# Conditioning rows spread by TensorE, spectra products 1024 wide, first units of up in another order

## The reference

```python
mod_x = silu(c) @ w_mod + b_mod          # and mod_c = silu(c_ctx) @ w_mod + b_mod
h = modulate(rms_norm(x, g_pre_mix), sh_m, sc_m)
x = x + gt_m * rms_norm(merge_heads(attention, retention, gate) @ w_out, g_post_mix)
x = x + gt_f * rms_norm((silu(a) * b) @ w_ffn_out, g_post_ffn)
# second block
x0, x1, v = split(short_conv(h @ w_in + b_in, sc_w, sc_b))
y = irfft(rfft(x1 * v) * rfft(kern)) + x1 * v * bias
x = x + g1 * ((x0 * y) @ w_out + b_out)
x = x + g2 * (silu(dwconv3x3(g)) * a) @ w_down      # a, g = split(modulate(rmsnorm(x)) @ w_up)
out = rmsnorm(x, final_g)
```

## Time and profile before

| | |
|---|---|
| median of three runs | 1423.12 us |
| profiled execution | 1426.7 us |
| its span, first to last instruction | 1424.9 us |
| TensorE busy | 1377.7 us, 97% |
| VectorE busy | 931.9 us, 65% |
| ScalarE busy | 540.2 us, 38% |
| GpSimd busy | 97.4 us, 7% |
| mean granted TensorE clock | 0.993 |

### The profile page before, as it was taken

How to read it: one execution, slowest core, us unless ns; L and a number is a source line. 1 busy time by engine, 2 the same in 40 slices (tenths; PEclk the granted TensorE clock), 3 DMA queues, 4 the chain that set the end, 5 groups by cost and what they waited for, 6 DMA issues and landing times.

```text
span 1424.9 us, 17227 instructions
## 1 busy us (share of the span) xinstructions
PE 1377.7 (97%) x6376; PEld 1102.7 (77%) x6376; DVE 931.9 (65%) x1277; ACT 540.2 (38%) x792; POOL 97.4 (7%) x119
## 2 busy tenths in 40 slices
PE   7899999999999999999999999999999999999996
PEld 5688887666888888888886577778887888888885
DVE  6756587786386666664134896999478888885222
ACT  3523253555462232323222654333453333333221
POOL 0002631000210000000110000000200000000010
PEclk9899999999999999999999999999999999999999
DMA  9434431032307565564521022220222322233311
GB/s 377 150 105 137 137 92 43 15 118 82 125 17 277 211 218 214 214 247 180 161 90 48 30 92 72 75 103 30 91 73 89 103 88 92 100 120 102 102 61 59
DMA packets 44803, 168.83 MB, mean 118 GB/s; under 512 B 5547, under 2 KB 6123, under 8 KB 43852
## 3 DMA queue, kind: packets, MB, share of 16 engines
q1 hardware_dynamic: 43340, 165.21, 33.2%
q0 software_dynamic: 1408, 2.89, 0.7%
HBM read 163.09 MB, written 2.10 MB: 116 GB/s over the span
## 4 chain that ended last, share of the span: by engine, by line
PE 81%; DVE 12%; ACT 2%; DMA 2%; issue 2%; SPq 0%; POOL 0%; DVEq 0%; ACTq 0%; POOLq 0%
PE PS L649 64%; PE PS L942 2%; PE PS L1009 2%; DVE tb L2060 2%; DVE wsp L639 1%; DVE sink L2116 1%; DVE H L2060 1%; PE PS L1204 1%; DMA mfirst<-mod_x 1%; PE PS L1301 1%; PE PS L1272 1%; DMA mring<-mod_c 1%; PE PS L1000 1%; PE PS L907 1%; DVE ca L2060 1%
## 5 line engine op out<-in xcount | busy, mean ns | idle before, releaser
L649 PE MATMUL PS<-H,wsp 128*128 128x512 f32 x3216 | 744.5, 392 | 12.1 <-DVE wsp L639 8.2
L649 PEld LDWEIGHTS PS<-H,wsp 128*128 128x128 f32 x3216 | 601.3, 188 | 148.8 <-DVE wsp L639 10.6
L639 DVE TENSOR_TENSOR wsp<-wraw,wsp 128x1024 fp32r<-128x1024 f32 (+1 forms) x172 | 223.1, 1299 | 335.0 <-ACT wsp L632 334.3
L632 ACT ACTIVATE wsp<-wraw 128x1024 fp32r<-128x1024 f32 (+1 forms) x172 | 191.8, 1118 | 468.8 <-PE PS L649 460.5
L649 PE MATMUL PS<-hid,wsp 128*128 128x512 f32 x1056 | 240.0, 389 | 0.0
L649 PEld LDWEIGHTS PS<-hid,wsp 128*128 128x128 f32 x1056 | 198.2, 188 | 41.7 <-issue 0.6
L2060 DVE SCALAR_TENSOR_TENSOR cva<-PS,dert,cva 128x441 f32<-128x441 f32 (+2 forms) x176 | 122.2, 694 | 5.5
L2262 DVE CUSTOM_DVE_ANT_0 sink<-mring,crow_t,colt 128x1024 bf16<-128x1024 f32 x56 | 71.8, 1281 | 11.4 <-DMA mring<-mod_c 10.8
L1969 POOL COPY acc<-sqb 128x512 f32<-128x512 f32 x4 | 3.9, 972 | 850.0 <-ACT sqb L1345 305.9
L1972 POOL TENSOR_TENSOR acc<-acc,sqb 128x512 f32<-128x512 f32 x20 | 34.1, 1707 | 184.3 <-ACT sqb L1947 82.6
L1690 ACT ACTIVATE hid<-hv 128x512 f32 (+1 forms) x22 | 13.9, 632 | 81.2 <-DVE hv L2535 81.2
(11 more groups left out here) (333 smaller groups left out, 1490.8 us busy)
## 6 DMA issues: line engine op xcount, KB each, us to landing
mring<-mod_c SPq DMA_DIRECT2D x56, 512.0 KB, 4.7
wraw<-w_ffn_in SPq DMA_DIRECT2D x44, 512.0 KB, 3.7
wraw<-w_up SPq DMA_DIRECT2D x44, 512.0 KB, 3.5
wraw<-w_hy_in SPq DMA_DIRECT2D x24, 512.0 KB, 3.5
wraw<-w_w_in SPq DMA_DIRECT2D x22, 512.0 KB, 3.5
wraw<-w_ffn_out SPq DMA_DIRECT2D x16, 704.0 KB, 4.0
wraw<-w_down SPq DMA_DIRECT2D x16, 704.0 KB, 4.0
mfirst<-mod_x SPq DMA_DIRECT2D x12, 512.0 KB, 16.6
```

What stands on the lines that cost most here:

```text
L632: nc.scalar.activation(split_parts(name, i, r)[0], wraw[:, g % RAW, 0:n], ACT.Copy).then_inc(w_hi, 1)
L639: nc.vector.tensor_tensor(part_lo, wraw[:, g % RAW, 0:n], part_hi.bitcast(F32), ALU.subtract).then_inc(w_lo, 1)
L649: mm = nc.tensor.matmul(psum, wsp[:, o % 2, a, wk * P:(wk + 1) * P], h[:, b, kt, :], start=first and kt == kts[0] and (a, b) == (0, 0), st ...
```

## The change

Three edits that don't touch each other.

At the start SP issues one row of each of the two conditioning rows to a single partition (`crow_r`, 8 KB), then `ones`, then `colt`. TensorE multiplies the first row of `ones` (a column of 1/1024 for each partition) by that row, four matmuls of 512 columns, which puts the rows divided by 1024 on all partitions in four PSUM banks; ScalarE's silu reads them with a scale of 1024. VectorE's work is the same.

In the spectra the product is made as four operations, two of 1024 columns, in which the filter's real or imaginary part is read twice by a stride of zero, and two of 512. The final sums are two of 1024 columns.

In the first units of up the sum over the second half's squares is split: tile 6's stands after two channel tiles, tile 7's after three, where both stood after five. ScalarE takes the root of the second half after all eight high parts of the first, spreads the splits of units 2 and 3 among the high parts of the second half, and loads the table of silu at the end. VectorE adds the residual of tile 7 one step earlier.

```diff
+        crow_r = sb("crow_r", o_r + 66 * K, [1, 2, D])
...
-        zp = [zA[:, 0, :], zA[:, 1, :], sb("zp2", o_t + 11 * K, [P, 512]), sb("zp3", o_t + 13 * K, [P, 512])]
+        zB = sb("zB", o_t + 11 * K, [P, 2, 512])
...
+        def spectra(c, f, pair):
+
+            return KS[:, c, (1, 0, 2, 3)[2 * f + pair], :, :]
...
+            sp.dma_start(crow_r[:, :, :], crow[0:1, 0:3:2]).then_inc(s_crow, 16)
+            sp.dma_start(ones[:, :], mats[0]).then_inc(s_crow, 16)
             sp.dma_start(colt[:, :], cols).then_inc(s_cols, 16)
-            for v in range(2):
-                sp.dma_start(crow_t[:, v, :], crow[:, 2 * v]).then_inc(s_crow, 16)
...
-            sp.dma_start(ones[:, :], mats[0]).then_inc(s_small, 16)
...
+            pe.wait_ge(s_crow, 32)
+            for b in range(4):
+                nc.tensor.matmul(PS[:, b, :], ones[0:1, :], crow_r[0:1, b // 2, b % 2 * 512:b % 2 * 512 + 512],
+                                 start=True, stop=True).then_inc(c_row, 1)
             pe.wait_ge(silu_c, 1)
             for m in range(3):
                 modulation(m)
-            pe.wait_ge(s_small, 16)
             squares_total(0)
...
-            def half_total(half):
+            def half_total(half, tiles=(6, 7)):
 
                 cs, bank = half_of(half * KT), 6 - half
-                pe.wait_ge(n_acc, acc_base(6) + 6)
-                nc.tensor.matmul(PS[:, bank, 0:HL], ones[:, :], acc[:, cs], start=True, stop=False)
-                for n in (6, 7):
+                if tiles[0] == 6:
+                    pe.wait_ge(n_acc, acc_base(6) + 6)
+                    nc.tensor.matmul(PS[:, bank, 0:HL], ones[:, :], acc[:, cs], start=True, stop=False)
+                for n in tiles:
...
                 pe.wait_ge(o_ev, 8)
-                tiles(range(0, 5), 0)
-                half_total(1)
-                tiles(range(5, KT), 0)
+                tiles(range(0, 2), 0)
+                half_total(1, (6,))
+                tiles(range(2, 3), 0)
+                half_total(1, (7,))
+                tiles(range(3, KT), 0)
                 tiles(range(KT), 1)
...
-            act.wait_ge(s_crow, 32)
             for v in range(2):
-                SC.activation(crow_t[:, v, :], crow_t[:, v, :], ACT.Silu).then_inc(crow_on, 1)
+                act.wait_ge(c_row, 2 * v + 2)
+                SC.activation(crow_t[:, v, :], PS[:, 2 * v:2 * v + 2, :].rearrange("p a b -> p (a b)"),
+                              ACT.Silu, scale=float(D)).then_inc(crow_on, 1)
...
             half_root(0)
-            half_highs(0, 3)
+            half_highs(0, 2)
             half_out(7, 1)
-            half_highs(3, 4)
+            half_highs(2, 4)
             half_square(7, 1)
-            half_highs(4, 6)
+            half_highs(4, KT)
             half_root(1)
-            half_highs(6, KT)
+            half_highs(KT, KT + 4)
             split_hi(act, "up", 2, after=ORD["hy_out"] + 7)
+            half_highs(KT + 4, 2 * KT)
             split_hi(act, "up", 3, after=ORD["hy_out"] + 8)
-            half_highs(KT, 2 * KT)
+            SC.preload_act_table(ACT.Silu)
...
-                z_re, z_im = zs[:, 2 * d, :], zs[:, 2 * d + 1, :]
-                k_re, k_im = spectrum(k // 2, f, 2 * d), spectrum(k // 2, f, 2 * d + 1)
-                re, im = zp[2 * d][:, :], zp[2 * d + 1][:, :]
-                VE.tensor_tensor(re, z_re, k_re, ALU.mult)
-                own(VE.tensor_tensor(im, z_im, k_im, ALU.mult))
-                VE.tensor_tensor(re, re, im, ALU.subtract)
-                VE.tensor_tensor(z_re, z_re, k_im, ALU.mult)
-                own(VE.tensor_tensor(z_im, z_im, k_re, ALU.mult))
-                own(VE.tensor_tensor(z_re, z_re, z_im, ALU.add))
+                z, y = zs[:, 2 * d:2 * d + 2, :], (zA, zB)[d]
+                k_re, k_im = [spectrum(k // 2, f, 2 * d + part).unsqueeze(1).to_broadcast([P, 2, 512])
+                              for part in range(2)]
+                VE.tensor_tensor(y[:, :, :], z, k_re, ALU.mult)
+                own(VE.tensor_tensor(z, z, k_im, ALU.mult))
+                VE.tensor_tensor(y[:, 0, :], y[:, 0, :], z[:, 1, :], ALU.subtract)
+                own(VE.tensor_tensor(y[:, 1, :], y[:, 1, :], z[:, 0, :], ALU.add))
...
-                VE.tensor_tensor(to[0], zp[0][:, :], zp[2][:, :], ALU.add)
-                VE.tensor_tensor(to[2], zp[0][:, :], zp[2][:, :], ALU.subtract)
-                VE.tensor_tensor(to[1], zs[:, 0, :], zs[:, 2, :], ALU.add)
-                VE.tensor_tensor(to[3], zs[:, 0, :], zs[:, 2, :], ALU.subtract).then_inc(z_y, 1)
+                VE.tensor_tensor(to[0], zA[:, :, :], zB[:, :, :], ALU.add)
+                VE.tensor_tensor(to[1], zA[:, :, :], zB[:, :, :], ALU.subtract).then_inc(z_y, 1)
...
                 half_low(i0 + 1)
+                if i0 == 0:
+                    half_residual(7, 1)
                 for i in range(i0 + 2, i0 + KT):
                     if i + 2 < i0 + KT:
                         half_scaled(i + 2)
                     half_low(i)
-                    if i == 2:
-                        half_residual(7, 1)
```

More of the change, by code:

```diff
@@ L267, in build @@
         s_crow = sem("s_crow")
+        c_row = sem("c_row")
         s_hyc = sem("s_hyc")
@@ L2177, in _ @@
             scaled(1, Xc, "a_ctx", (0, 1, 2, 3), LC)
-            dve.wait_ge(s_small, 64)
+            dve.wait_ge(s_small, 48)
             own(VE.tensor_tensor(centre[:, :], ident[:, :], bones[:, :], ALU.subtract))
@@ L2693, in z_products @@
                 f = k % 2
-                z_re, z_im = zs[:, 2 * d, :], zs[:, 2 * d + 1, :]
-                k_re, k_im = spectrum(k // 2, f, 2 * d), spectrum(k // 2, f, 2 * d + 1)
-                re, im = zp[2 * d][:, :], zp[2 * d + 1][:, :]
-                VE.tensor_tensor(re, z_re, k_re, ALU.mult)
-                own(VE.tensor_tensor(im, z_im, k_im, ALU.mult))
-                VE.tensor_tensor(re, re, im, ALU.subtract)
-                VE.tensor_tensor(z_re, z_re, k_im, ALU.mult)
-                own(VE.tensor_tensor(z_im, z_im, k_re, ALU.mult))
-                own(VE.tensor_tensor(z_re, z_re, z_im, ALU.add))
-            def z_final(k):
-                to = [spectrum(k // 2, k % 2, part) for part in range(4)]
-                VE.tensor_tensor(to[0], zp[0][:, :], zp[2][:, :], ALU.add)
-                VE.tensor_tensor(to[2], zp[0][:, :], zp[2][:, :], ALU.subtract)
-                VE.tensor_tensor(to[1], zs[:, 0, :], zs[:, 2, :], ALU.add)
-                VE.tensor_tensor(to[3], zs[:, 0, :], zs[:, 2, :], ALU.subtract).then_inc(z_y, 1)
+                z, y = zs[:, 2 * d:2 * d + 2, :], (zA, zB)[d]
[5 more added lines that the diff above has]
+                own(VE.tensor_tensor(y[:, 1, :], y[:, 1, :], z[:, 0, :], ALU.add))
+            def z_final(k):
+                to = [spectra(k // 2, k % 2, pair) for pair in range(2)]
+                VE.tensor_tensor(to[0], zA[:, :, :], zB[:, :, :], ALU.add)
+                VE.tensor_tensor(to[1], zA[:, :, :], zB[:, :, :], ALU.subtract).then_inc(z_y, 1)
                 dve.wait_ge(z_y, k + 1)
```

## The result

The changed kernel took 1417.94 us (median of seven runs, 1415.8 to 1420.34), the kernel before 1424.73 in the same comparison (seven runs, 1422.78 to 1427.13). The medians differ by 6.8 us. The ratio is 0.995, with a 95% interval of 0.9941 to 0.9959, which is 7.1 us, 5.8 to 8.4. The forecast was 1416.9.

The account below looks back on a forecast made before the run. TensorE was taken to bound the kernel with 81% of the chain of waits, VectorE 12%. Start 1.5, spectra 1.7 and up 3.0 sum to 6.2 us, from the median of 1423.12 to 1416.9; range 1413.9 to 1420.4.

Parts of the forecast that it names:

- the 1074.5: Up's end: TensorE's long last piece, at 1078.18 before, starting later than this would show the forecast wrong.
- the start: Program start: VectorE reaches the unit it waited for at 20.07 instead of 21.55; gain 1.5 us.
- up: First units of up: shorter `tiles`, hidden table load, VectorE setting the wait for unit 5; gain 3.0 us, bounds 1.8 and 4.3.
- the price of the four products: Start: TensorE's four new float32 products, priced by the first four sums over squares, take 5.8 us.
- The first rival: Start: TensorE's rate stays at 1.71 us for all four products, the start gives nothing, 1418.4 us; chance 0.17.
- The landing's term: Start: the matrix's next unit lands 2.0 to 2.9 us earlier, taken as 2.2, so at 19.35.
- The transfer term: Start: the small transfer `ones`, issued at 1.21, lands at 3.9, at most about 4.1.
- The spectra: Between 884 and 982 us: each product takes VectorE 0.25 less, final sums 0.12 less; gain 1.7 us.
- The term of `tiles`: First units of up: first `tiles` matmul to the next full unit takes 15.5 us instead of 17.3; 1.8 gained.
- The bound of 4.3: First units of up: the upper bound of the gain, with TensorE ready for unit 5 at 1073.9.
- The operand that is read slowly: Spectra rival: a stride of zero halves VectorE's rate, 12.8 us more, 1429.7 us; chance 0.04.
- The clock's fall: Rival: TensorE's lower clock moves onto the chain or lasts longer, costing 3.4 us, 1420.3 us; chance 0.08.

Follow-up runs that it names:

- rows_12: Changed kernel with eight more one-row products behind the four at the start, into free banks; 1428.06 us in one run, the kernel before 1427.32 beside it.
- rows_full: Changed kernel with the four start products over all 128 rows, 127 of them zero; 1420.81 us in one run, the kernel before 1427.32 beside it.
- rows_apart: Changed kernel with VectorE taking the first row's sums of its first three units before the second row's; 1418.53 us (0.9946), again 1419.45 (0.9954).

## Why the prediction was right, and where it was off

The time came out 1.0 us above the forecast and in its range, and the sign and the places were right. As a gain it was 6.8 us by the medians for 6.2, since the kernel before took 1.6 us more in this comparison than the median from which the forecast started. The three places in the trace give 7.07. TensorE's long last piece starts at 1069.31, well before the 1074.5 that would have shown the forecast wrong, but 1.8 of that is the part that no edit gave. Two terms had the wrong size, in opposite directions: the start gave 0.9 less than forecast and up 1.6 more. That the sum came so close is in part luck.

**The start (forecast 1.5, traced 0.63, timed nothing).** The step that failed is the price of the four products, 1.71 + 1.71 + 1.49 + 0.86. It was taken from sums over 128 rows, in which TensorE's rate rose; in products with one active row it didn't (`rows_12`, `rows_full`), and four took 7.2. That VectorE and not the landing then decides, and that some 9.32 us lie between its start and the unit that it had waited for, held: 20.93 less 11.71 is 9.22. The first rival had the mechanism: rate unchanged through all four and hardly anything gained. Its sign, a start of VectorE's after 12, did not show, because `ones` came early and made up for part of it. The landing's term was somewhat too large: in the three profiles in which it can be seen the landing came 1.96, 1.63 and 1.41 earlier than in the kernel before, for 2.2 with a lower bound of 2.0. The transfer term erred to the other side: `ones` came 1.86 after its issue, not 2.7. The Trainium skill, DMA: Bandwidth & Descriptors, under "Anatomy of one DMA", has a fixed cost of about 2.0 us. The trace about agrees, with 1.86.

**The spectra (1.7, traced 1.88).** Right in each step: 3.72 a product, 1.22 for an operation with the spread operand, no surcharge, and the 0.68 in front of the inverse transform just fitted. Its second half was forecast for 979.1. Its start can't be seen in a row of 128 matmuls, but the unit behind it starts 4.34 earlier than before (991.74 for 996.08), which puts it at 978.01. Of the 4.34, 0.63 come from the start, 1.83 from the stretch without edits and 1.88 from the spectra.

**Up (3.0, traced 4.56).** The term of `tiles` was mis-sized, 15.5 where 13.74 was measured. I priced a matmul by a piece of the chain, 1.77 us for 12, 0.1475 each; the 78 in one run take 10.17, 0.130 each. 96 at 0.130 and three sums are 13.8. So in the kernel before some 3.6 us of the 17.31 went to waits and to what each break adds to the matmuls around it, not 1.8, and all of that went. Its timeline shows four waits there, of which the prediction read one, the 1.22 of the earlier trace rows. The others are

```profile
1044.79 1.77 PE L1009 MATMUL PS<-H,upw 128*128 128x256 f32 x12 [0.15 <-DVE H L2060]
...
1052.48 0.98 PE L1009 MATMUL PS<-H,upw 128*128 128x256 f32 x6 [1.01 <-DVE H L2060]
...
1053.67 5.58 PE L1009 MATMUL PS<-H,upw 128*128 128x256 f32 x42 [0.21 <-DVE H L2060]
```

and the last row, 42 in 5.58 or 0.133 each, would have given the right price. The order of waits held: silu at once, VectorE in front of unit 5, a wait of 1.58 for 1.3. With 3.57 for `tiles` instead of 1.8, the same steps give 3.57 + 1.28 = 4.85, less the 0.25 by which the load is not hidden: 4.6, and 4.56 came through. The bound of 4.3 fell with it, since it too was counted from 1.8. VectorE sets it, but 1.6 us earlier than forecast.

**The other rivals.** The operand that is read slowly is out (1.22). The clock's fall did move between executions, but not by the change: the stretch at 230 us costs 1.3 us on TensorE's path, and with the same code there some profiles have it and some don't. Runs of the changed kernel lie up to 2.4 us from their median; such a stretch is large enough to make much of that, which was not shown for the runs without a profile.

What stays open is why the clock falls in one execution and not in the next, whether the start's 0.6 to 0.8 us in the traces is there in the time as well, and whether `rows_apart` is better or worse than the change by a few tenths, which five runs cannot tell.

## What to carry to other kernels

Price a matmul by the long uninterrupted run of its shape (here 0.130 us), not by a short piece of the chain (0.1475), and price the first matmuls of a program by ones with as many active rows. When two profiles differ by more than the edited places, look at a kernel with the same code there before giving the rest to the change. A wait of TensorE's behind a saturated engine moved on here when one operation was taken out of turn; I would expect only less work ahead of it to remove it, which was not tried.

## What the runs showed of the hardware

- TensorE did not rise from its lower level (1.2 GHz) in 20.8 us of back-to-back products with one active row (`rows_12`: 1.73 us for 512 columns of float32, first and last alike). With 128 rows, 127 of them zeros, four such products took 5.77 us (`rows_full`), and the small matmuls behind them ran at twice the rate.
- The profile's granted clock reads 1.00 in the first microseconds although durations are twice the later ones. This is the changed kernel from 5 to 10 us, with the clock third from the end, in passes of some 0.85 us each:

```profile
5.00:10.00 5.00, 5.00 (x7) 1.66 (x5) 0.00 (x0) 1.25 (x2) 0.00 (x0) 1.00 1.02 379
```

- A float32 operand read twice by a stride of zero in its middle axis cost VectorE nothing: 1.22 us for 1024 columns with and without it, and 1.14 from one operation to the next.
- A table load cost ScalarE 1.28 us and nothing around it. At the start of the changed kernel an activation ends at 11.67, the load runs from 11.69, and the next activation begins at 12.98.
- With the same code, TensorE's granted clock from 230 to 235 us was 0.66 in some executions and 1.00 in others (16 matmuls in 3.63 or 2.05 us).
